# Up products on unnormalised x with the reciprocal rms on their relu, a first up group of eight plain products, and an earlier residual sum, in a hybrid transformer step

## The reference, cut to what matters

```python
def rmsnorm(x, g):
    y = x * lax.rsqrt(jnp.mean(jnp.square(x), -1, keepdims=True) + EPS)
    return y * g

x = x + mixed                                  # mixed = concat(...) @ w_out, 2048 x 2048
u = rmsnorm(x, norm2_g) @ w_up                 # 2048 x 8192
x = x + jnp.square(jax.nn.relu(u)) @ w_down    # 8192 x 2048
return rmsnorm(x, final_norm_g)
```

## Time and profile before

| | us |
|---|---|
| median of three runs | 2398.95 (2397.71 to 2398.97) |
| the profiled execution | 2395.72 |
| its span, first to last instruction | 2393.9 |
| mean granted TensorE clock | 0.985 of full |
| TensorE busy | 2318.3 (97%) |
| DVE, ScalarE, POOL busy | 1608.8, 936.9, 871.2 |

### The profile page before, as it was taken

How to read it: one execution, slowest core, us unless ns; L and a number is a source line. 1 busy time by engine, 2 the same in 40 slices (tenths; PEclk the granted TensorE clock), 3 DMA queues, 4 the chain that set the end, 5 groups by cost and what they waited for, 6 DMA issues and landing times.

```text
span 2393.9 us, 46062 instructions
## 1 busy us (share of the span) xinstructions
PE 2318.3 (97%) x18396; PEld 2244.5 (94%) x18396; DVE 1608.8 (67%) x2332; ACT 936.9 (39%) x1213; POOL 871.2 (36%) x357
## 2 busy tenths in 40 slices
PE   8999999999999999969999999999999999999997
PEld 7979899999999899969999999999899999999997
DVE  5258725555555543388888888888877777777775
ACT  5141222222222422245555555555433333333344
POOL 3413323223233444333333333333333333333354
PEclk9999989999999999979999999999999999999998
DMA  6523323333332354415555555666976556656631
GB/s 220 132 78 93 92 63 86 92 85 92 93 92 75 100 170 122 128 36 177 198 196 193 194 194 194 200 200 200 324 244 209 170 193 230 208 188 203 206 121 73
DMA packets 349079, 368.77 MB, mean 154 GB/s; under 512 B 16818, under 2 KB 301682, under 8 KB 348018
## 3 DMA queue, kind: packets, MB, share of 16 engines
q1 hardware_dynamic: 336866, 352.16, 46.4%
q10 hardware_dynamic: 12064, 14.53, 1.7%
HBM read 288.85 MB, written 77.80 MB: 153 GB/s over the span
## 4 chain that ended last, share of the span: by engine, by line
PE 90%; DVE 5%; issue 2%; ACT 1%; DMA 1%; POOL 0%; SPq 0%; ACTq 0%; DVEq 0%
PE product L925 51%; PE product L636 31%; PE banks L667 6%; PE banks L664 1%; DVE s_up L1758 1%; DMA x_in<-in_x_prompt_dram 1%; DVE xr L1900 0%; DMA raw<-in_w_up_dram 0%; PE product L667 0%; DVE xr L1752 0%; DVE a_lo L1707 0%; DVE xr L1893 0%; DVE xr L1776 0%; ACT w_hi L1224 0%; DVE score L1524 0%
## 5 line engine op out<-in xcount | busy, mean ns | idle before, releaser
L596 POOL TENSOR_TENSOR w_lo<-raw,w_hi 128x1024 fp32r<-128x1024 f32 x193 | 500.5, 2599 | 820.4 <-ACT w_hi L1224 819.4
L925 PE MATMUL product<-s_up,w_hi 128*128 128x260 f32 x3600 | 653.7, 284 | 16.6 <-ACT c_b L1060 8.1
L925 PE MATMUL product<-s_dn,w_hi 128*128 128x260 f32 x3584 | 652.2, 284 | 15.7 <-DVE xr L1893 11.3
L925 PEld LDWEIGHTS product<-s_up,w_hi 128*128 128x128 f32 x3600 | 556.6, 189 | 21.0 <-issue 14.2
L925 PEld LDWEIGHTS product<-s_dn,w_hi 128*128 128x128 f32 x3584 | 552.6, 188 | 20.7 <-issue 15.6
L563 POOL TENSOR_TENSOR w_lo<-w_raw,w_hi 128x1024 fp32r<-128x1024 f32 (+1 forms) x134 | 323.4, 2416 | 659.2 <-ACT w_hi L1057 659.2
L925 PE MATMUL product<-s_up,w_lo 128*128 128x260 f32 x1800 | 508.3, 282 | 0.0
L925 PE MATMUL product<-s_dn,w_lo 128*128 128x260 f32 x1792 | 506.9, 283 | 0.0
L636 PE MATMUL product<-a_hi,w_hi 128*128 128x260 f32 (+1 forms) x2144 | 440.4, 287 | 7.7 <-DVE a_lo L1416 3.9
L636 PE MATMUL product<-a_hi,w_lo 128*128 128x260 f32 (+1 forms) x2144 | 434.1, 284 | 0.0
L636 PE MATMUL product<-a_lo,w_hi 128*128 128x260 f32 (+1 forms) x2144 | 433.7, 284 | 0.0
(11 more groups left out here) (275 smaller groups left out, 1929.5 us busy)
## 6 DMA issues: line engine op xcount, KB each, us to landing
raw<-in_w_up_dram SPq DMA_DIRECT2D x64, 1024.0 KB, 9.6
raw<-in_w_down_dram SPq DMA_DIRECT2D x64, 1024.0 KB, 5.6
s_dn<-hidden_combinations SPq DMA_DIRECT2D x112, 520.0 KB, 8.8
w_raw<-in_w_in_dram SPq DMA_DIRECT2D x100, 512.0 KB, 3.9
hidden_combinations<-h_hi SPq DMA_DIRECT2D x31, 910.0 KB, 3.8
hidden_combinations<-h_lo SPq DMA_DIRECT2D x31, 910.0 KB, 6.8
w_raw<-in_w_out_dram SPq DMA_DIRECT2D x32, 512.0 KB, 4.0
x_transposed<-xr ACTq DMA_DIRECT2D x2, 2080.0 KB, 7.8
```

What stands on the lines that cost most here:

```text
L596: nc.gpsimd.tensor_tensor(ring(w_lo, g, n), block_of(g, i, j), ring(w_hi, g, n).bitcast(F32), ALU.subtract).then_inc(s_lo, 1)
L925: mm_last = nc.tensor.matmul(out, w[:, k, col:col + P], s[:, h, k, :], start=(first and k == 0 and part == 0), stop=(last and k == kn - 1 ...
```

## The change

**No normalised x.** x times the gain is split without the reciprocal rms. ScalarE squares each output tile into PSUM (square_of), DVE only sums the squares (sum_square). The high and low parts of the quarters of each tile are made as soon as the tile is there (quarters_high, quarters_low); for the first eight tiles DVE then also replaces x21 by x11 - x21. The order of positions in s_up changes with it (up_slot). The two low parts that POOL made (low_s) go to DVE.

**Group 0** starts right after the last output product. The ten products for the sum of squares and those that spread the rms now stand behind its first and its third product.

**The scaling.** ScalarE copies the spread reciprocal rms to SBUF (rb_s), and its first half also into PSUM bank 1. DVE puts relu and the factor on in one instruction, maximum with 0 and then multiplication: in group 0 scaled_first, from group 1 on scaled_up, on the last product's bank, on two columns of c_b together, and on the third. The relus on ScalarE go. squared follows high_unit(g, 2), ahead of the evacuation of position 0 and of high_unit(g, 3), which had stood ahead of it.

**Down.** add_x stands behind add_down(g, 1, 1). s_dn has 14 slots in another order (down_slot), t_s, out_s, yt, sq2 and out_t lie elsewhere, and the first weight sum of the last chunk comes behind add_down(g, 4, 1). At the first down group product 1 waits for scaled_up(31), which reads its bank.

```diff
@@ sync
                 else:
-                    sp.wait_ge(s_used, base_unit(UPG - 1) + (pos // 2, (7 + pos) // 2)[c] + 1)
+                    sp.wait_ge(s_used, base_unit(UPG - 1) + (pos // 2 + 1 if c == 0 else 7))
@@ tensor
+            def sum_squares():
+                pe.wait_ge(s_n2, KT + 1)
+                for tb in range(5):
+                    tok = slice(tb * P, min(tb * P + P, T))
+                    last = mm(B[0:tok.stop - tok.start, 0, tb:tb + 1], ssum[:, tok], ones[:, 0:1])
+                last.then_inc(s_n2m, 1)
...
                 for tok_half in range(2):
+                    if tok_half == 0 and n < 2:
+                        pe.wait_ge(s_evac, TILE_OUT + KT - 1 + n)
...
+                    last = product(bank(((2, 0), (3, 1))[tok_half][j]), w_unit, s_up[:, ((4, 5), (6, 0))[tok_half][i]], 8,
+                                   i == 0, i == 1, ready=ready)
+                    if n == 0 and tok_half == 0:
+                        sum_squares()
+                    elif n == 1 and tok_half == 0:
+                        spread_rms()
...
+                            elif pos:
+                                pe.wait_ge(s_sc, UPG - 1)
@@ scalar
+            def square_of(t):
+                act.wait_ge(s_evac, TILE_OUT + t + 1)
+                if t >= 2:
+                    act.wait_ge(s_n2, t)
+                act_fn(B[:, 2 * (t % 2):2 * (t % 2) + 2, 0:HALF_COLS], halves(xr[:, t, :]), ACT.Square).then_inc(s_sqx, 1)
+
+            def quarters_high(t):
...
+                nc.scalar.copy(quarters_part(t, 0), quarters_of(t)).then_inc(s_ah, 1)
...
             for g in range(1, UPG):
                 x_bank = last_x(g)
-                high_unit(g, 2)
                 if g > 1:
-                    taken(g - 1, 6, r21[:, :], last_x(g - 1), ACT.Relu)
-                    relu_rest(g - 1)
+                    high_unit(g, 2)
+                    squared(g - 1)
+                taken(g, 0, c_b[:, 0, :], x_bank)
                 high_unit(g, 3)
-                squared(g - 1)
-                taken(g, 0, c_b[:, 0, :], x_bank)
                 high_unit(g, 4)
                 high_unit(g, 5)
                 taken(g, 2, c_b[:, 1, :], x_bank)
                 high_unit(g, 6)
                 taken(g, 3, c_b[:, 2, :], 3)
+                if g == 1:
+                    squared(0)
@@ vector
+            def scaled_up(g):
+                dve.wait_ge(s_used, base_unit(g) + 7)
+                dve.wait_ge(s_sqh, g)
+                v.scalar_tensor_tensor(out=r21[:, :], in0=G[:, last_x(g), 0:HALF_COLS], scalar=0.0,
+                                       in1=rb_s[:, thalf(1)], op0=ALU.max, op1=ALU.mult).then_inc(s_r6, 1)
+                dve.wait_ge(s_rv, 3 * g)
+                if g == 1:
+                    dve.wait_ge(s_rbc, 3)
+                v.scalar_tensor_tensor(out=c_b[:, 0:2, :], in0=c_b[:, 0:2, :], scalar=0.0,
+                                       in1=G[:, 1, 0:HALF_COLS].unsqueeze(1).to_broadcast([P, 2, HALF_COLS]),
+                                       op0=ALU.max, op1=ALU.mult)
+                v.scalar_tensor_tensor(out=c_b[:, 2, :], in0=c_b[:, 2, :], scalar=0.0,
+                                       in1=rb_s[:, thalf(1)], op0=ALU.max, op1=ALU.mult).then_inc(s_sc, 1)
...
             sum_blocks(1, 1)
             sum_blocks(1, 2)
-            low_s(2, x11, 7)
+            low_s(2, x22, 3)
+            dve.wait_ge(s_used, base_unit(0) + 4)
+            scaled_first(a21[:, :], 0, slice(0, HALF_COLS), 0)
+            scaled_first(c22a[:, :], 1, slice(0, 240), 1)
+            scaled_first(c22b[:, :], 1, slice(240, HALF_COLS), 1)
             low_sum(1, 2)
-            low_s(4, x21, 8)
+            low_s(3, x11, 4)
             low_sum(1, 1)
             for g in range(1, UPG):
                 if g > 1:
+                    scaled_up(g - 1)
                     low_sum(g, 2)
                     low_sum(g, 1)
                 take(g, 0)
                 sum_blocks(g, 3)
                 low_sum(g, 3)
+                if g == 1:
+                    low_s(5, x12, 5)
                 sum_blocks(g, 4)
-                combine_hidden(g - 1)
+                if g > 1:
+                    combine_hidden(g - 1)
                 low_sum(g, 4)
                 take(g, 1)
                 sum_blocks(g + 1, 1)
                 take(g, 2)
                 sum_blocks(g + 1, 2)
+                if g == 1:
+                    combine_hidden(0)
                 hidden_low(g - 1)
...
+            scaled_up(UPG - 1)
             low_sum(UPG, 2)
...
+                if UPG + 5 <= g < UPG + 5 + KT:
+                    add_x(g - UPG - 5, 14 * (g - UPG) + 4)
                 add_down(g, 2, 0)
...
-                if more:
+                if more and g + 1 != LAST_CHUNK:
                     sum_blocks(g + 1, 1)
                 add_down(g, 4, 0)
                 add_down(g, 4, 1)
                 if more:
+                    if g + 1 == LAST_CHUNK:
+                        sum_blocks(g + 1, 1)
                     sum_blocks(g + 1, 2)
...
-                if UPG + 5 <= g < UPG + 5 + KT:
-                    add_x(g - UPG - 5, 14 * (g - UPG) + 12)
                 add_down(g, 6, 0)
```

More of the change, by code:

```diff
@@ L1027, in _ @@
                             pe.wait_ge(s_rd, 14 * (g - UPG) + 2 * prev + sub + 1)
-                        last = product(bank(b), (ring(w_hi, g, n), ring(w_lo, g, n)), s_dn[:, c % 2, pos], 4,
+                        last = product(bank(b), (ring(w_hi, g, n), ring(w_lo, g, n)), s_dn[:, down_slot(c, pos)], 4,
                                        pos in (0, 1, 3), True, col=P * sub)
@@ L1232, in _, with high_s @@
+            high_unit(0, 1)
+            square_of(KT - 2)
             gained(13)
-            high_unit(0, 1)
+            quarters_high(13)
+            def high_s(pos, x):
+                nc.scalar.copy(s_up[:, up_slot(pos), 0, :, :], x).then_inc(s_sh, 1)
+            x11, x21 = xr[:, 0:8, thalf(0)], xr[:, 0:8, thalf(1)]
+            x12, x22 = xr[:, 8:16, thalf(0)], xr[:, 8:16, thalf(1)]
+            square_of(KT - 1)
+            act.wait_ge(s_used, TAKEN0_UNITS)
+            act.wait_ge(s_s3, 8)
@@ L1256, in _ @@
+            for n in range(2):
+                nc.scalar.copy(rb_s[:, thalf(n)], B[:, n, 0:HALF_COLS]).then_inc(s_rbc, 1)
             high_unit(1, 0)
-            high_s(4, x21, 6)
-            high_s(5, x12, 8)
+            act.wait_ge(s_xn, 1)
+            high_s(2, x22)
+            act.wait_ge(s_xn, 2)
+            high_s(3, x11)
             high_unit(1, 1)
-            for n, (dst, b) in enumerate(((c_b[:, 0, :], 2), (r21[:, :], 3), (c_b[:, 1, :], 0), (c_b[:, 2, :], 1))):
-                act.wait_ge(s_used, base_unit(0) + (3 if n < 2 else 4))
-                act_fn(dst, G[:, b, 0:HALF_COLS], ACT.Relu).then_inc(s_r0, 1)
+            act.wait_ge(s_xn, 3)
@@ L1775, in _, with low_s, scaled_first @@
-            dve.wait_ge(s_xn, 6)
-            v.tensor_tensor(x11, x22, x11, ALU.subtract).then_inc(s_xn, 1)
-            dve.wait_ge(s_xn, 7)
-            v.tensor_tensor(x12, x11, x12, ALU.add).then_inc(s_xn, 1)
+            def low_s(pos, x, made):
+                dve.wait_ge(s_sh, made)
+                v.tensor_tensor(s_up[:, up_slot(pos), 1, :, :], x, s_up[:, up_slot(pos), 0, :, :].bitcast(F32),
+                                ALU.subtract).then_inc(s_sl, 1)
+            def scaled_first(out, b, cols, tok_half):
+                v.scalar_tensor_tensor(out=out, in0=G[:, b, cols], scalar=0.0,
+                                       in1=rb_s[:, tok_half * HALF_COLS + cols.start:tok_half * HALF_COLS + cols.stop],
+                                       op0=ALU.max, op1=ALU.mult).then_inc(s_v0, 1)
```

259 lines of the change are left out of this document (126 added, 133 removed).

## The result

The changed kernel takes 2401.68 us (median of 20 runs, 2398.87 to 2406.91), the kernel before, run beside it, 2398.48 (20 runs, 2395.77 to 2400.74). The ratio is 1.0014, with a 95% interval of 1.0008 to 1.0021. It is slower by an amount under the 0.2% that I had called no change, where I had forecast 5.3 us less. The profiled execution is the slowest of its 20, 2406.91 us.

A forecast was written before the change was run, and what follows sets the result against it. TensorE, busy 97%, was taken as the bound. Up's end +5.7 (transition included), entry +1.5, residual sums -12.5 make -5.3 us: 2390.4 from the profiled 2395.72, 2393.6 with 3.2 for the median; range 2373 to 2405.

The forecast's parts named there:

- Transition: From the last output product to the end of group 2: ends at +78.6 instead of +94.3, 15.7 us gained.
- The walk: Step-by-step timing of groups 0 to 2 with their stalls, ending at +78.6, good to 4 us either way.
- Up loop: Groups 3 to 31: period 21.0 us instead of 20.26, so up products end at +687.6; 5.7 us lost, transition included.
- The ring: Up-loop circle of waits among TensorE, ScalarE, POOL and DVE: items sum to 21.22 us per group, taken as 21.0.
- Entry to down: Start of the down groups: DVE has 1.32 us more in front, product 1 waits for a scaling; 1.5 us lost, 0 to 4.
- Residual sums: Down groups: moving add_x off the group's end gains 11.4 to 13.1 us over 16 groups, taken as 12.5.
- Rival 1: Up loop stays on TensorE at 20.26 us per group, 21.5 us less than forecast: 2372; chance 0.17.
- Rival 2: Up loop slower, handoffs in full and third scaling caught by POOL's lock: period from 21.2, at 21.5 2408 us; chance 0.2.
- Rival 3: Down groups: the wait at the group's end is for low_sum's high half, add_x only filled it: 2406; chance 0.03.
- the main case: Up period between 20.8 (2388 us) and 21.2 (2399 us), with 4 us around it for the transition; chance 0.6.

The follow-up runs named there:

- experiment 6: Kernel after, with unread matmuls filling TensorE's two long waits (ahead of group 1's product 5 and group 2's product 1): 2397.70 us, ratio 0.9993 to the kernel before.
- experiment 2: Kernel after, with DVE's three scalings of a group ahead of hidden_low instead of behind it: 2387.24 us, ratio 0.9950 to the kernel before.
- experiment 3: Kernel after, with ScalarE's copy for product 3 ahead of the squares in groups 2 to 31: 2385.99 us, ratio 0.9942 to the kernel before.
- experiment 4: Kernel after, with two more unread scalings (260 and 240 columns) per group on DVE: 2420.05 us, ratio 1.0083 to the kernel before.
- experiment 7: Kernel after, with the last chunk's first weight sum back in its place through another order of buffer slots: 2397.93 us, ratio 0.9995 to the kernel before.
- experiment 8: Kernel after, with the edits of experiments 2, 3, 5 and 7 together: 2372.68 us, ratio 0.9890 to the kernel before.
- experiment 5: Kernel after, with ScalarE's order of evacuation and copies changed in group 1 alone: 2399.76 us, ratio 1.0002 to the kernel before.
- experiment 1: Kernel before, with only the residual sum (add_x) moved to just behind the addition of product 1's second half: 2386.83 us, ratio 0.9948 to the kernel before.

## Why the prediction was wrong

I forecast -5.3 us. The medians differ by +3.2, the four stretches of the two profiles by +4.1. The terms of the sum, in its order, against the profiles:

1. **Transition, -15.7 forecast, -11.9 measured: the step that failed first.** The walk named the right stalls, at 0.2 to 0.3 us. (Its 31.9 for product 2 without a stall should read 31.6, 25.8 and two products; nothing rests on it.) The failing sentence is that a stall of 3.9 us "may also cost clock [...] and that lies within the walk's 4". I saw the mechanism, priced product 5 at 2.9 more, and put nothing into the sum. Product 5 took 2.6 more, and behind the second stall another 1.6 went: 3.8 us over the forecast in the profile, and 3.6 come back when the stalls are filled (experiment 6). By the Trainium skill ("TensorE: Matmul & The Clock Gate", "What's actually happening") stalls of this size could each be followed by a slow stretch. The trace agrees for all those of 3.3 us and more; at the 2.6 and 1.6 us measured here the sum would have been about 4 us higher, an estimate.
2. **Up loop, +21.5 forecast (29 x 0.74), +23.8 measured.** The ring was right in every item, to 0.06 us (the row that gave its 3.15 is of product 2 of group 1, not of product 4, and has as many matmuls); experiments 2, 3 and 4 break or stretch it and the period follows. The failing step is the last: "TensorE's stalls in this ring are of 0.1 to 0.6 us, in which the product before has hardly drained, so I take 21.0". The restart and the tail of the product cost 3.25 of the 3.29, though TensorE stands still there for hardly 0.2 us; that argument had no row behind it and cost 0.10 x 29 = 2.9 us, of which 0.5 is given back at the loop's start. The ring of 21.22, taken as summed, was nearer than the number I made of it.
3. **Entry to down, +1.5 forecast, +1.4 measured.** The scalings in front of DVE's list cost 1.2 of it, as I had it; the wait that they lengthen is at product 0's second half, not at product 1.
4. **Residual sums, -12.5 forecast, -9.2 measured.** The move by itself takes 11.5 off the down groups (experiment 7 against before). My rows gave 11.4 to 13.1 and I took 12.5: 1.0 too much, since the groups run at 20.35 to 20.37 and not at the 20.26 of the other end. The failing sentence for the rest: the last chunk's sum moved behind an addition is "covered by the idle time before the next; were it not, 1.2 once". It stalled TensorE for 2.18 us, since the next sum then met POOL's low half (3.21, against 1.72 before) and two sums stood in front of one addition. It is 3.6 us where the clock falls behind it.

3.8 + 2.4 + 1.0 + 2.2 = 9.4, which carries -5.3 to the profiles' +4.1. The medians' +3.2 is 0.9 less, well within the 8 us that the executions of the kernel after lie apart. None of the four was a mechanism that I had missed; each was a cost that I had seen and rounded down, or a gain that I had rounded up, all in the same direction. They had nothing to do with each other, but the same habit made them: where a cost had a bound from zero up and a cover that seemed likely, I took zero, or the low side.

**The rivals.** Rival 1 (the loop stays on TensorE, 0.17) did not come: the ring decides. It was right about DVE's load and wrong about the order: once the ring is broken the loop runs at 20.28 (experiment 8). That this kernel also takes rival 1's 2372 is luck, since it holds experiments 5 and 7 as well, which bring 3.8 us at the end of group 2 and 2.2 in the down groups. Rival 2, the slower end, had its deciding point at a ring of 21.2; the ring is 21.10, and the third scaling meets POOL only in group 1 (1.63 us in the trace of after, at 1081.02), not in the steady loop. Rival 3 falls with experiment 1. In the rows of the loop DVE's raw sum and hidden_low end 1.09 and 1.91 us behind POOL's low halves, and the second low half waits for that sum. That is the exclusion of whole instructions that the Trainium skill ("SBUF — State Buffer", "Who interferes with whom") describes, and the trace agrees.

**The numbers.** The time lies in the range and in the part of the main case that I had called no change, 0.31. Between a gain of 15.7, a loss of 21.5 and a gain of 12.5, 52% for "faster" was too much: the walk was good to 4 us and the ring to 0.2 x 29 = 5.8, and a difference of 5.3 is inside either.

## What to carry to other kernels

A loop whose engines wait for each other in a circle has a period that can be summed from rows, item by item, and the sum should be used as it is; an engine at 87% busy says nothing about it. An edit that adds work to an engine with room is free only if it is put where that engine waits anyway: the same three scalings cost 0.84 us a group or hardly anything, by the place of two calls. And when several changes come as one, try each alone: here one moved call brings about 12 us, and the rest gave it back and more.

## What the hardware showed that I had not expected

- The lower clock behind a stall of TensorE: after 3.3 to 4.7 us of standing still in the transition it fell in every profile (0.50 to 0.86 in stretches of 5 us), costing 1.4 to 2.7 us. After 2.2 to 2.4 us it depends on the execution. Of the eight profiles of the kernel after and its variants three have it behind the stall ahead of product 2 of group 1 (2.37 to 2.40), and four of six behind the one of 2.18 in the down groups: behind 2.37 in the profile of after the clock stayed at 1.00 and behind 2.18 too, behind 2.18 in experiment 5 it was 0.69, and behind 2.40 in experiment 6 0.74:

```profile
1045.00:1050.00 5.00, 2.60 (x14) 0.74 0.00 0
```

  So such a stall has no single price. Why one execution shows it and the next does not, stays open.
- Filling a stall with matmuls that nobody reads made this kernel faster, since the product behind was on the path: 3.6 us in the trace for 48 of them.
- A second ring stands closely behind the first: 21.10, then 20.58 or 20.57 on average with either edit alone, 20.28 only with both. Either edit alone brought about six tenths of the 0.84 us, and neither showed the bound.
